# High and low halves of a narrow gate projection packed into one 128-wide weight, in a float32 block kernel on one Trainium2 core

## The reference, cut to what matters

```python
proj = h @ w_in                                   # 1024 x 3088; the last 16 columns are a_low
q, k, v, r, a_low = jnp.split(proj, splits, axis=-1)
log_a = jax.nn.log_sigmoid((a_low @ w_alpha_up + b_alpha)) / GLA_TAU   # w_alpha_up is 16 x 512
...
b = jnp.cumsum(log_a)                              # decays of queries, keys and state
```

## Time and profile before

| what | value |
|---|---|
| three runs | 1360.44, 1359.22 and 1360.1 us, median 1360.1 |
| the profiled execution | 1360.86 us by the clock of the runs |
| its span from first to last instruction | 1359.1 us |
| mean granted TensorE clock | 0.996 of full speed |
| busy: TensorE, VectorE, ScalarE, GpSimd | 98%, 67%, 53%, 9% |

### The profile page before, as it was taken

One profiled execution on the slowest core, in us unless ns is written; L12 is line 12 of the kernel. 1 busy time (PEld: TensorE's weight loads), 2 busy tenths in 40 slices (PEclk: granted clock), 3 DMA queues, 4 the chain that ended last, 5 costly groups with the idle time before them and its releaser, 6 DMA issues.

```text
span 1359.1 us, 23120 instructions
## 1 busy us (share of the span) xinstructions
PE 1337.8 (98%) x8826; PEld 1198.2 (88%) x8826; DVE 907.8 (67%) x1417; ACT 726.0 (53%) x1155; POOL 121.3 (9%) x123
## 2 busy tenths in 40 slices
PE   9999999999999999999999999999999999999998
PEld 8888989889987889999888889999988877999996
DVE  5757655557645647555567569777868775787776
ACT  6655544445334536444464457555557656665553
POOL 0002000002500000000001300000002233000000
PEclk9999999999999999999999999999999999999999
DMA  7535655555553456555554345555554411365551
GB/s 255 187 125 205 219 185 187 187 185 183 189 186 124 156 171 217 185 187 187 187 169 146 105 156 196 195 184 190 170 188 162 166 53 51 126 210 187 184 184 72
DMA packets 63887, 231.09 MB, mean 170 GB/s; under 512 B 7088, under 2 KB 7344, under 8 KB 63792
## 3 DMA queue, kind: packets, MB, share of 16 engines
q1 hardware_dynamic: 62208, 224.42, 49.2%
q10 hardware_dynamic: 1584, 5.31, 1.1%
HBM read 228.66 MB, written 1.05 MB: 169 GB/s over the span
## 4 chain that ended last, share of the span: by engine, by line
PE 89%; DVE 5%; ACT 2%; issue 2%; DMA 1%; POOL 1%; POOLq 0%; DVEq 0%; SPq 0%; ACTq 0%
PE ps L565 27%; PE ps L567 27%; PE ps L566 27%; DVE w_lo L1701 2%; PE ps L934 1%; DVE x_lo L1721 1%; ACT w_hi L1228 1%; PE ps L537 1%; PE ps L1094 1%; PE ps L1125 1%; DMA ring<-ws 1%; PE ps L1107 1%; ACT x_hi L1248 1%; PE ps L858 1%; PE ps L783 0%
## 5 line engine op out<-in xcount | busy, mean ns | idle before, releaser
L1701 DVE TENSOR_TENSOR w_lo<-ring,w_hi 128x1024 fp32r<-128x1024 f32 x424 | 514.8, 1253 | 174.2 <-ACT w_hi L1228 173.8
L1228 ACT ACTIVATE w_hi<-ring 128x1024 fp32r<-128x1024 f32 x424 | 429.5, 1052 | 232.8 <-PE ps L567 181.3
L565 PE MATMUL ps<-x_hi,w_hi 128*128 128x256 f32 x1600 | 455.0, 284 | 0.5 <-DVE x_lo L1721 0.5
L566 PE MATMUL ps<-x_lo,w_hi 128*128 128x256 f32 x1600 | 452.7, 283 | 0.0
L567 PE MATMUL ps<-x_hi,w_lo 128*128 128x256 f32 x1600 | 452.7, 283 | 0.0
L565 PEld LDWEIGHTS ps<-x_hi,w_hi 128*128 128x128 f32 x1600 | 306.8, 192 | 4.1 <-issue 3.0
L566 PEld LDWEIGHTS ps<-x_lo,w_hi 128*128 128x128 f32 x1600 | 306.9, 192 | 1.1
L567 PEld LDWEIGHTS ps<-x_hi,w_lo 128*128 128x128 f32 x1600 | 306.8, 192 | 0.0
L565 PE MATMUL ps<-w_hi,y_hi 128*128 128x512 f32 x560 | 220.3, 393 | 0.4 <-DVE y_lo L1753 0.4
L566 PE MATMUL ps<-w_lo,y_hi 128*128 128x512 f32 x560 | 218.3, 390 | 0.0
L567 PE MATMUL ps<-w_hi,y_lo 128*128 128x512 f32 x560 | 218.1, 389 | 0.0
(11 more groups left out here) (219 smaller groups left out, 1260.8 us busy)
## 6 DMA issues: line engine op xcount, KB each, us to landing
ring<-ws SPq DMA_DIRECT2D x424, 512.0 KB, 4.8
tab<-tables ACTq DMA_DIRECT2D x3, 550.0 KB, 5.3
rowg<-rows ACTq DMA_DIRECT2D x3, 512.0 KB, 6.2
h<-x SPq DMA_DIRECT2D x4, 256.0 KB, 6.1
out<-arena SPq DMA_DIRECT2D x4, 256.0 KB, 2.2
arena<-decay ACTq DMA_DIRECT2D x1, 768.0 KB, 8.6
sm<-small ACTq DMA_DIRECT2D x1, 642.0 KB, 4.7
arena<-narrow ACTq DMA_DIRECT2D x1, 296.0 KB, 2.9
```

Of the source, the lines that this page charges most:

```text
L565: mm(o, lh, rh, start=start, stop=False, skip_group_check=True)
L566: mm(o, lh, rl, start=False, stop=False, skip_group_check=True)
L1228: A(w_hi[:, q // 2 % RING, c:c + HALF], ring[:, q % RAW, :], ACT.Copy).then_inc(hi_ready, 1)
L1701: V.tensor_tensor(w_lo[:, g % RING, v], ring[:, q % RAW, :], w_hi[:, g % RING, v].bitcast(F32), ALU.subtract).then_inc(lo_ready, 1)
```

## The change

The narrow weight is now stored as 8 tiles of 128 x 128, 1024 columns in all, with the 16 columns repeated at columns 0, 32, 64 and 96 of each tile and zeros between. The 16 x 512 weight of the second product is repeated at partitions 0, 32, 64 and 96 of `small`. What is made of them:

- ACT loads the weight (512 KB) in front of the second MLP, at the end of retention, into a free part of the arena.
- After `sumsq(5)` ACT copies it to `gl_w` (128 x 1024) and the second weight to `gl_alpha` (128 x 512), both float32r. They lie in `y_hi`, which the MLP before uses, so ACT waits for the end of that MLP.
- After `fold(5)` DVE turns rows 96 to 111 of `gl_alpha` and columns 32 to 47 of each tile of `gl_w` into low parts. TensorE waits for this (`n_ready` at 4) in front of the narrow projection.
- The projection is 16 products in place of 24. Rows 0, 64 and 96 on of its result are the high weight's, rows 32 on the low weight's.
- DVE scales all 128 rows into `gl_low32`, ACT rounds them into `gl_low`, DVE turns rows 64 to 79 into low parts (`gla_low_in` 1, 2 and 3).
- The second product is four float32r products over all 128 rows.
- `spread(5)` moves from in front of `transposed(G_GLA + 2)` to between its two runs.
- `n_hi` and `n_lo` lose the 128 GLA columns (592 to 464).

```diff
 # TensorE
             def gla_logits():
-                pe.wait_ge(gla_low_in, 1)
+                pe.wait_ge(gla_low_in, 3)
...
-                        c = S_ALPHA + (2 * i + j) * P
-                        r = mm(ps[:, (7, 4)[i], j * T:(j + 1) * T], sm[0:16, c:c + P], gl_low, start=True, stop=True,
+                        c = (2 * i + j) * P
+                        r = mm(ps[:, (7, 4)[i], j * T:(j + 1) * T], gl_alpha[:, c:c + P], gl_low, start=True, stop=True,
...
             natural(G_GLA, (0, 1), first=5)
-            pe.wait_ge(n_ready, 2)
+            pe.wait_ge(n_ready, 4)
             for k in range(KT):
-                r = mm3(ps[:, 4, 0:T], n_hi[:, 16 * k:16 * k + P], n_lo[:, 16 * k:16 * k + P],
-                        x_hi[:, k, :], x_lo[:, k, :], k == 0, k == KT - 1)
+                w = gl_w[:, P * k:P * (k + 1)]
+                mm(ps[:, 4, 0:T], w, x_hi[:, k, :], start=k == 0, stop=False, skip_group_check=True)
+                r = mm(ps[:, 4, 0:T], w, x_lo[:, k, :], start=False, stop=k == KT - 1, skip_group_check=True)
             r.then_inc(gla_small_proj, 1)
-            spread(5)
-            transposed(G_GLA + 2, 5)
+            transposed(G_GLA + 2, 5, mid=lambda: spread(5))
             transposed(G_GLA + 3, 6, mid=gla_logits)
 # ScalarE
+            act.dma_start(gl_w32, narrow[:, 0:N_LOW]).then_inc(narrow_in, 16)
             norm(3, G_RET + 30, G_RET + 31)
...
             act.dma_start(rowg[:, :], rows[1:2, :].partition_broadcast(P)).then_inc(row_in, 16)
+            act.wait_ge(narrow_in, 32)
+            act.wait_ge(done, G_MLP[1] + 32)
+            A(gl_w, gl_w32, ACT.Copy)
+            A(gl_alpha, sm[:, S_ALPHA:S_ALPHA + 512], ACT.Copy).then_inc(n_ready, 1)
             refill(G_GLA)
...
             spread(5, scale)
+            act.wait_ge(gla_low_in, 1)
+            A(gl_low, gl_low32, ACT.Copy).then_inc(gla_low_in, 1)
             refill(G_GLA + 2)
 # VectorE
             fold(5)
+            dve.wait_ge(n_ready, 3)
+            w = gl_alpha[96:112, :]
+            V.tensor_tensor(w, sm[96:112, S_ALPHA:S_ALPHA + 512], w.bitcast(F32), ALU.subtract)
+            raw, w = (v.rearrange("p (k c) -> p k c", c=P)[:, :, 32:48] for v in (gl_w32, gl_w))
+            V.tensor_tensor(w, raw, w.bitcast(F32), ALU.subtract).then_inc(n_ready, 1)
             refill(G_GLA)
             refill(G_GLA + 1)
...
-            V.tensor_tensor(gl_low, ps[0:16, 4, 0:T], scale[0:16, :], ALU.mult).then_inc(gla_low_in, 1)
+            V.tensor_tensor(gl_low32, ps[:, 4, 0:T], scale, ALU.mult).then_inc(gla_low_in, 1)
...
+            dve.wait_ge(gla_low_in, 2)
+            v = gl_low[64:80, :]
+            V.tensor_tensor(v, gl_low32[64:80, :], v.bitcast(F32), ALU.subtract).then_inc(gla_low_in, 1)
             gla_unit(0)
```

More of the change, by code:

```diff
@@ L51 @@
 S_TOTAL = S_ALPHA + 512
-N_LOW = KT * 16
+N_LOW = KT * P
 N_GATE = KT * 48
-N_TOTAL = N_LOW + N_GATE + 80
+N_TOTAL = N_GATE + 80
 TAB = 1100
@@ L165, in gl_total @@
             return v.rearrange("p a (b c) -> p a b c", c=2)
-        gl_low = gl_l[0:16, 0, :]
+        gl_low32, gl_w32 = gl_x[:, 0, :], region(14848, N_LOW)
+        y_flat = y_hi[:, :, :].rearrange("p a t -> p (a t)")
+        gl_w, gl_alpha, gl_low = y_flat[:, 0:N_LOW], y_flat[:, N_LOW:N_LOW + 512], y_lo[:, 0, :]
         ns_kd = region(0, 2, NSA_KV, T)
@@ L1152, in _ @@
             for k in range(KT):
-                c = N_LOW + 48 * k
+                c = 48 * k
                 r = mm3(ps[:, 1, 0:T], n_hi[:, c:c + P], n_lo[:, c:c + P], y_hi[:, k, :], y_lo[:, k, :],
@@ L1395, in _ @@
             refill(G_SB + 14)
-            act.dma_start(narrow_raw, narrow).then_inc(narrow_in, 16)
+            act.dma_start(narrow_raw, narrow[:, N_LOW:N_LOW + N_TOTAL]).then_inc(narrow_in, 16)
             act.dma_start(sm[:, S_CONV:S_TOTAL], small[:, S_CONV:S_TOTAL]).then_inc(rest_loaded, 16)
@@ L2555 @@
     small[:, S_PE + 16:S_PE + 32] = a["cmp_pe_v_2"].reshape(16, P).T
-    small[0:16, S_ALPHA:S_ALPHA + 512] = a["gla_w_alpha_up_2"][0]
+    for r in range(0, P, 32):
+        small[r:r + 16, S_ALPHA:S_ALPHA + 512] = a["gla_w_alpha_up_2"][0]
     small[:, S_ID:S_ID + P] = np.eye(P)
-    narrow = np.concatenate([a["gla_w_in_2"][0][:, 3072:3088].reshape(KT, P, 16).transpose(1, 0, 2).reshape(P, -1),
+    low = np.zeros((P, KT, P), np.float32)
+    for c in range(0, P, 32):
+        low[:, :, c:c + 16] = a["gla_w_in_2"][0][:, 3072:3088].reshape(KT, P, 16).transpose(1, 0, 2)
+    narrow = np.concatenate([low.reshape(P, -1),
                              win[:, D:D + 48].reshape(KT, P, 48).transpose(1, 0, 2).reshape(P, -1),
-                             np.zeros((P, N_TOTAL - N_LOW - N_GATE), np.float32)], 1)
+                             np.zeros((P, N_TOTAL - N_GATE), np.float32)], 1)
     rows = np.stack([a["g_final"], a["gla_norm_2"][0].reshape(D), a["norm_final_2"]])
```

## The result

| | before | after |
|---|---|---|
| median of 12 runs each | 1360.11 us | 1362.85 us |
| lowest and highest | 1358.37, 1360.83 | 1361.61, 1364.04 |
| profiled execution, its span | 1360.86, 1359.1 | 1362.15, 1360.4 |

What follows compares the result with a forecast made beforehand. TensorE, busy 98% of the span, was taken to bound the kernel. +1.1 us at full clock and +1.5 for the low clock gave +2.6, moving the median from 1360.1 to 1362.7 us; range 1360.9 to 1364.5.

Steps and rivals of the forecast that it cites:

- The sum at full clock: TensorE, start of GLA: wait, 16 products and moved transposes +2.70, second product gives back 1.6; +1.1 us, bounds 0.8 to 1.6.
- The projection and the second product: TensorE, GLA gate: 8 fewer products save 0.94 us; four dense products in place of plain float32 save 1.6 us.
- The new wait: TensorE before the projection: DVE's subtractions after fold(5) delay its start 4.30 us, to 703.86; bounds 703.6 to 704.3.
- The clock: TensorE at the new pause: the clock falls in or right behind it; 16 slow products cost 1.5 us, ends 0 and 2.8.
- The rival of a low stretch of 6.8 us: Low clock as long as at 1052: 28 dense products lose 2.5 us; +3.6, so 1363.7; chance 0.27.
- What lies beside: Six side effects on DVE, ACT, loads and later waits, all costed at nothing, up to 1 us if one is wrong.
- (5): The 512 KB load in ACT's queue at the end of retention has room before the ring needs it; no cost.
- (6): Smaller n_hi and n_lo in the first MLP: under 0.15 us on ACT and DVE, costed at nothing.
- The chain to the second product: Longer scale, copy and subtraction steps on DVE and ACT, done by about 711; TensorE asks at 714.7, 3 us to spare.
- The rival of an early preparation: Halves ready before the projection at 699.6: no wait, -3.0 us, so 1357.1, faster by 0.22%; chance 0.03.
- the bracket of 0.49: TensorE's 0.49 us pause before the two transposes of spread, waiting for DVE's rfold; counted as gained if it goes.
- the forecast alone: One short stretch at the low clock after the new pause: 1362.7 us, own range 1362.2 to 1363.2; chance 0.48.

Runs made afterwards that it cites:

- e5: The kernel of e1 with the old products put back in number and form, without the gate's low parts; 1358.93 us against 1359.96 before.
- e6: The kernel of e1 with the gate's own steps ahead of the weight pieces on ScalarE and VectorE; 1356.97 us against 1359.96 before.
- e2: The changed kernel with only the order in two queues moved, ACT's copies and DVE's subtractions earlier; 1357.92 us against 1359.78 before.
- e1: The changed kernel with the halves of both gate weights made some 25 us earlier, in free tiles; 1357.44 us against 1359.78 before.
- e3: The changed kernel with four dummy float32 products in front of TensorE's wait for the halves; 1361.02 us against 1359.78 before.
- e8: The changed kernel with two dummy products in front of the wait for the halves; 1362.54 us against 1359.96 before.
- e4: The kernel before with only the two transposes of the scale moved between the first unit's two runs; 1359.08 us against 1359.78 before.
- e7: The kernel of e6 with two dummy products in front of the sparse attention's wait; 1356.52 us against 1359.96 before.

## Why the prediction was right

The time, 1362.7 against a measured 1362.85, and its two terms held: the wait and the clock. That the agreement is as close as 0.15 us is in part luck. The sum at full clock was 0.28 too small by the marks, and the medians moved 0.14 less than the marks.

- *The projection and the second product.* Summed at 0.94 and 1.6; together 2.59 by e5 against e6.
- *The new wait.* Its place and cause were right: DVE behind `fold(5)` (e2 moves the work ahead of it and the pause shrinks to 0.60), and not ACT, whose copies end at 702.29, while `fold(5)` ends at 703.50. e1 and e2 move both engines' work, so it is the timeline that tells the two apart. Its length was 0.24 short: TensorE starts 4.77 us behind S, where 703.86 - 699.33 = 4.53 was forecast. I had let both subtractions overlap their neighbours by 0.08. They did not: the first starts at 703.53, at the end of the one before it (703.34 + 0.16), and the second at 704.23, at the end of the first. The next one, `w_lo`, overlaps again. The Trainium skill states this (VectorE: DVE Perf Modes, section Two Vector instructions with no wait between them): an instruction whose operands start in another group of 32 partitions than those before it starts only when the earlier ones are finished. `gl_alpha[96:112]` is such a one, so is the subtraction behind it, which starts at partition 0 again, and the trace agrees: no overlap at either, here and in e1, e2, e3, e5, e6 and e8. By the 0.08 of each, an estimate, it would have made the sum 0.16 longer; `rfold` itself came 0.03 later behind S.
- *Full clock.* +1.1 was forecast, +1.38 is measured (e3); 0.24 of the difference is the wait, and the first product after the pause takes 0.22 (704.58 to 704.80) in place of 0.12, which was in no term. The transposes and the second product gave back some 0.08 of this.
- *The clock.* It fell, for 3.41 us, and the low stretch was all dense: 17 starts from 705.15 to 708.69 in 3.54 us, which at 0.12 take 2.04. That is 1.50, as forecast, and the marks of after and e3 give 1.50 too. No row of the kernel before gave the length of such a stretch, the only one there was 6.8 us long; that the 16 products I took are nearly the 17 measured is luck in part. By the penalty of the Trainium skill (TensorE: Matmul & The Clock Gate, section Terms), half of the time at the low clock, it would be 1.7, an estimate; the trace has 1.5, because a product of 256 columns takes 0.12 at full clock and not half of 0.213. At 1052 in the kernel before it fell while TensorE was idle; here it fell behind the return, and the whole low stretch was dense. The rival of a low stretch of 6.8 us cannot be excluded for executions without a profile. Seven of the 12 have a mean granted clock of 0.996, as the profiled one, and took 1361.61 to 1363.39 us; five have 0.995 and took 1363.08 to 1364.04. From these means I estimate at least 2 us more at the low clock in the five; whether at 705 or at 1056, no run shows.
- *What lies beside.* No cost shows in the changed kernel for any of the six: the only pauses of TensorE from S to M are the 4.38 and the 1.00, M - S is explained to 0.1 by the terms above, and the pauses ahead of S, where (5) and (6) lie, are no longer than before. The chain to the second product had 3.8 us to spare (done at 713.13, the product at 716.95), where I had counted 3. But this cover came from the late start itself: in e1, where TensorE comes to the second product 5.7 us sooner behind S than after (11.42 against 17.14), both that chain and DVE's tree were late.
- *The rival of an early preparation* was priced at -3.0. e1 and e6, which make it true, gave -2.3 and -3.0 in the medians. It had used the bracket of 0.49 for the transposes, and e4 shows 0.69.
- *The verdict.* The forecast gave 0.50 to no change and 0.46 to slower; measured are 0.22%, just beyond the bound of 0.2, with an interval that reaches from 0.14 to 0.3, so on which side of the bound it lies is not settled. The range that I gave for the forecast alone began at 1362.2; by its own terms (0.8 + 1.5 over 1360.1) it should have begun at 1362.4.

## What to carry to other kernels

Fewer products of the same size are worth what their count says (2.54 us summed, 2.59 measured), but the operands that they need must be made where the engine that makes them is idle, and a new wait must be placed behind nothing that waits itself: the same instructions give 1362.85 or 1357.92 us by their place in two queues. When an independent product is made dependent, ask which wait it was covering. A pause of TensorE like those of 1.9 to 4.4 us here is to be priced with the low clock behind it (1.5 us where dense products followed, more than the 0.94 that the projection saved), and an engine that is made 3 us earlier needs its next suppliers looked at again.

## What the runs showed of the hardware

- The granted clock fell after pauses of 1.92 (e3, at 1053), 2.11 (e8, at 1056), 2.22 (e7), 2.20 to 2.30 (before, after, e1, e2, e4, e5 and e6, at 1049 to 1055), 2.67 (e8) and 4.38 us (after), and not after 0.96 (e3), 1.33 (e1) and 1.46 (before, e6). The pauses near 1050 were followed by thin products and one more pause of 0.5 to 0.65 us, so their length is not all that differs. The clock fell between 0.3 us ahead of TensorE's return (before, 1052.2 against 1052.48) and 2.4 us behind it (e3, 1055.55 against 1053.19). Each low stretch in these profiles, apart from the one at the very end, lasted 3.41 us, or 6.83 (before, e2).
- Dummy products that fill 3.6 of the 4.6 us kept the clock at 1.00 in the profile of e3; 1.9 us of them did not in that of e8.
- The first product of 256 columns after a pause takes 0.22 us in place of 0.12 (after 0.60 us in e2, 0.96 in e3, 4.38 in after).
- DVE's subtraction on partitions from 96 on overlaps neither the instruction before it nor the one behind it, both of which start at partition 0 (703.50 to 703.53 and 704.22 to 704.23 in after); `rfold` and the `w_lo` behind it, both from partition 0, overlap by 0.08 us before (702.91 against 702.99).
